# Down weights loaded four rows to a partition, and gate and up columns read four apart, in the expert stage of a two-layer backbone

## What is computed

```python
def expert_block(args):
    xblk, e = args
    hid = jax.nn.silu(xblk @ w_gate[e]) * (xblk @ w_up[e])   # [rows, 1024] @ [1024, 512], twice
    return hid @ w_down[e]                                    # [rows, 512] @ [512, 1024]
```

## Time and profile before

| What | Value |
|---|---|
| Median of 3 runs | 1149.04 us (1146.02 to 1150.01) |
| The profiled execution's own time | 1149.13 us |
| Its span, first to last instruction | 1147.1 us |
| PE busy | 1044.6 us (91%) |
| DVE busy | 621.8 us (54%) |
| ACT busy | 206.4 us (18%) |
| HBM read over the span | 314.36 MB |
| Mean granted clock of TensorE, share of full | 0.976 |

### The profile page before, as it was taken

One profiled execution on the slowest core, in us unless ns is written; L12 is line 12 of the kernel. 1 busy time (PEld: TensorE's weight loads), 2 busy tenths in 40 slices (PEclk: granted clock), 3 DMA queues, 4 the chain that ended last, 5 costly groups with the idle time before them and its releaser, 6 DMA issues.

```text
span 1147.1 us, 36219 instructions
## 1 busy us (share of the span) xinstructions
PE 1044.6 (91%) x14841; PEld 651.5 (57%) x14842; DVE 621.8 (54%) x1596; ACT 206.4 (18%) x543; POOL 140.6 (12%) x215
## 2 busy tenths in 40 slices
PE   4899989999698989999996999999988999999977
PEld 1344445554244767777773444444446777777752
DVE  1278877874358434444442886653584444444426
ACT  1212255550111000000001511021120000000010
POOL 0001100000001212122223000000012111221221
PEclk9999999999799999999997999999999999999998
DMA  8997952239534999999968994883349999999575
GB/s 319 350 345 273 340 196 74 74 147 241 179 122 169 372 421 415 421 374 418 426 266 305 336 352 159 300 310 105 118 167 382 420 414 381 376 406 424 185 298 193
DMA packets 97733, 331.91 MB, mean 289 GB/s; under 512 B 15593, under 2 KB 28305, under 8 KB 89361
## 3 DMA queue, kind: packets, MB, share of 16 engines
q1 hardware_dynamic: 66672, 289.05, 65.6%
q10 hardware_dynamic: 24672, 22.74, 6.0%
q0 software_dynamic: 6336, 19.41, 4.6%
HBM read 314.36 MB, written 25.18 MB: 296 GB/s over the span
## 4 chain that ended last, share of the span: by engine, by line
PE 70%; DMA 12%; DVE 8%; issue 3%; ACTq 2%; SPq 2%; ACT 2%; DVEq 0%; POOLq 0%
PE PS L1630 20%; PE PS L1640 12%; PE PS L1732 9%; PE PS L1425 8%; PE PS L1544 7%; DMA ring<-in_e_down_dram 5%; PE PS L1447 4%; DMA expert_rows<-RE 3%; PE PS L1473 3%; DMA RFW<-in_ln_b_dram 2%; PE PS L1459 2%; DMA ring<-in_a_wqkv_dram 2%; ACTq L601 1%; PE PS L1474 1%; PE PS L1688 1%
## 5 line engine op out<-in xcount | busy, mean ns | idle before, releaser
L1630 PE MATMUL PS<-ring,RE 128*32 128x128 f32 x6912 | 210.1, 273 | 12.3 <-issue 9.4
L1630 PEld LDWEIGHTS PS<-ring,RE 128*32 128x32 f32 x6912 | 194.6, 110 | 31.4 <-issue 22.7
L1217 DVE TENSOR_TENSOR RE<-RE,PS 128x64 f32<-128x64 f32 x160 | 35.4, 221 | 174.9 <-ACT RE L722 174.3
L1640 PE MATMUL PS<-ring,RE 128*32 128x256 f32 x1504 | 109.5, 387 | 10.2 <-DMA ring<-in_e_down_dram 4.8
L722 ACT ACTIVATE RE<-PS 128x64 f32<-128x64 f32 x160 | 35.7, 223 | 461.0 <-PE PS L1630 436.2
L1544 PE MATMUL PS<-ring,UR 128*128 128x512 f32 x256 | 115.0, 604 | 0.8 <-ACT UR L612 0.8
L1732 PE MATMUL PS<-ring,UR 128*128 128x512 f32 x256 | 111.1, 593 | 0.9 <-ACT UR L766 0.9
L1630 PE MATMUL PS<-UR,RE 128*32 128x128 f32 x3200 | 95.7, 273 | 3.5 <-issue 3.3
L1425 PE MATMUL PS<-ring,UR 128*128 128x512 f32 x224 | 98.2, 592 | 0.5 <-DMA ring<-in_a_wqkv_dram 0.5
L1630 PEld LDWEIGHTS PS<-UR,RE 128*32 128x32 f32 x3200 | 90.2, 110 | 9.9 <-issue 6.6
L531 POOL DMA_INDIRECT RE<-tokens,gcol x80 | 79.5, 993 | 60.4 <-POOL gcol L545 60.4
(11 more groups left out here) (278 smaller groups left out, 1136.0 us busy)
## 6 DMA issues: line engine op xcount, KB each, us to landing
ring<-in_w_ada_dram SPq DMA_DIRECT2D x24, 2048.0 KB
ring<-in_e_up_dram SPq DMA_DIRECT2D x22, 2048.0 KB
ring<-in_e_gate_dram SPq DMA_DIRECT2D x22, 2048.0 KB
ring<-in_e_down_dram SPq DMA_DIRECT2D x20, 2048.0 KB
RFW<-in_e_down_dram SPq DMA_DIRECT2D x12, 2048.0 KB, 19.2
UR<-in_e_up_dram SPq DMA_DIRECT2D x10, 2048.0 KB
UR<-in_e_gate_dram SPq DMA_DIRECT2D x10, 2048.0 KB
expert_rows<-RE ACTq DMA_DIRECT2D x320, 32.0 KB
```

The costliest lines, as they stand in the source:

```text
L1217: V_.tensor_tensor(hid[:, cut], gs[:, cut], PS[:, h, 64:128], ALU.mult).then_inc(loop, 1)
L1630: ins = mm(PS[BLK * q:BLK * q + BLK, h, 0:P].rearrange("p (g b i) -> p g b i", g=2, b=2), xT[:, k, :], wgu[:, :, k, 2 * h:2 * h + 2, q, :] ...
L1640: ins = mm(PS[BLK * q:BLK * q + BLK, 5, 0:256], hidT[:, BLK * k:BLK * k + BLK], wd[:, k, 256 * q:256 * q + 256], start=(k == 0), stop=(k = ...
```

## The change

Down rows are now loaded four consecutive ones to a partition: partition p holds rows 4p to 4p+3, one piece of 16 KB, as gate and up have it. For the hidden columns to come out in that order, the gate and up products take column 4(32 q + i) + b where they took column 128 b + 32 q + i. The moving operand's innermost loop i thus steps by four floats (16 bytes) where it stepped by one, and the loop b outside it by one float where it stepped by 128.

```diff
@@ load_expert
-                    src = e_down[l, e].rearrange("(k p) n -> p k n", p=P)
+                    src = e_down[l, e].rearrange("(p k) n -> p k n", k=FC)
@@ the first load of the spare slot
-                             e_down[l, src].rearrange("(k p) n -> p k n", p=P)).then_inc(w_in[b], 16)
+                             e_down[l, src].rearrange("(p k) n -> p k n", k=FC)).then_inc(w_in[b], 16)
@@ expert
-                    wgu = pair.rearrange("p g (k b q i) -> p g k b q i", k=DC, b=FC, q=CG)
+                    wgu = pair.rearrange("p g (k q i b) -> p g k b q i", k=DC, b=FC, q=CG)
```

## The result

The changed kernel takes 1395.19 us (1392.55 to 1399.57, 4 runs) against 1149.53 us of the kernel before (1146.02 to 1154.22, 4 runs): a ratio of 1.2138, 95% interval 1.2083 to 1.2193. It is slower by a fifth. The forecast was 1411.

The account below looks back on a forecast made before the run. The prediction took PE, with line 1630's column stream, to bound the kernel. To 1149.1 us it added 273 for slower reads, less 11.5 given back, loads and the rest 0: 1411 us, range 1144 to 1425.

Parts of the forecast that it names:

- What bounds: Whole kernel: PE busy 91% of the span; line 1630 is a stream at 0.86 ns a column.
- The reads: Line 1630: 16-byte steps raise a column from 0.86 to 1.70 ns, bounds 0.86 to 1.84.
- The term of 273 us: Line 1630: 2528 groups, each 0.108 us longer through the slower reads, all on the path.
- What the slowing gives back: Expert stages: late-weight waits of 4.8 and 5.4 us and a slow pass of 1.3 us go, together -11.5 us.
- The 5.4 us at line 1681: Wait for the first weights after layer 0's experts, expected to go as expert blocks grow by 3.4 us.
- The loads: Down loads in 16 KB pieces gain 2%: 0 under a slowed PE, bounds 0 to -4.3 us.
- the step is free on PE: Rival at line 1630: PE hides the fetch, leaving only the loads' gain; 1145 to 1149 us, chance 0.38.
- the cover: Down loads' 4.3 us gain lies wholly under the slowed PE, so it counts 0 in the sum.
- What was to stay as it was: Down product, SiLU and transposes keep instructions, addresses and lengths: 0.
- the factor: Rival at line 1630: strided columns cost 1.6 times plain ones, 1.38 ns; 1305 us, chance 0.08.
- one memory in turn: Rival at line 1630: four side-by-side products served in turn, 3.4 ns a column; 1970 us, chance 0.04.

Follow-up runs that it names:

- e2_reads_only: Kernel before with only the change's gate and up reads (16-byte steps), down loads as before: 1396.27 us, ratio 1.2159.
- e1_loads_only: Changed kernel with the gate and up reads of before, so only the down loads differ from the kernel before: 1194.83 us, ratio 1.0397.
- e4_pairs: Changed kernel with a read's two loops swapped, taking two neighbouring floats from each 16-byte place: 1184.01 us, ratio 1.0310.
- e9_halves: Kernel before with each gate and up load issued as two, in pieces of 8 KB instead of 16: 1149.13 us, ratio 1.0005.
- e3_two_rows: Kernel before with down rows two to a partition (8 KB pieces), gate and up read in 8-byte steps: 1153.47 us, ratio 1.0033.
- e12_pairs_halves: e4_pairs with each gate and up load issued as two, in 8 KB pieces: 1137.50 us, ratio 1.0047.

## Why the prediction was right, point by point

**What bounds.** Right: PE's stream at line 1630 was the path. What it lost was paid in full, less what the slowing gave back.

**The reads.** Right in kind, a little low in size. The step took 1.70 ns a column from DVE's rows; PE has 1.81, inside the bounds of 0.86 to 1.84. The term of 273 us is 291.9 in the page, 18.9 more. That a fetch costs a time and not a factor, the ground for choosing between 1411 and 1305, is borne out by the table above: PE's 1.81 ns is DVE's price (1.67 to 1.84) and not 1.6 times PE's own 0.86. Of the note on cachelines in the Trainium skill (SBUF — State Buffer, "Door 1"), the first half agrees with the trace: each new line pays, and two accesses to one line absorb it (0.90 ns). The second, that 4 fp32 are strided for free, does not: a step of 3 fp32 already costs 1.37 ns and one of 4 costs 1.81.

**What the slowing gives back.** Too small: -11.5 us stood there, of waits for down weights and for the first weights after layer 0. The runs have -48.5. Of these, 31.7 us are idle time before expert products, of which the page of before puts 19.0 under "issue"; the 4.8 us of waits for down weights went as said. The other 16.8 us are line 1640's, for whose length the prediction had only 1.3 us. Some of its passes were slow in the kernel before, as this one of 3.47 us, behind a stop of 2.45 us and at a granted clock of 0.53:

```profile
405.93 3.47 PE L1640 MATMUL PS<-RFW,RE 128*32 128x256 f32 x32 [2.45 <-issue]
...
405.90:409.30 3.40, 3.37 (x36) 1.89 (x40) 0.77 (x3) 0.22 (x1) 0.42 (x1) 0.53 1.06 430
```

In the changed kernel no pass takes more than 2.2 us from its first start to its last end, and the granted clock is 1.00 in both stages, where it was 0.98 and 0.99. What the stops of about 2 us named "issue" were, and why they vanish under a slower PE, no run shows.

The 5.4 us at line 1681 did not come back. The wait for weights is gone, but behind it stood one for DVE (line 1194) of 3.8 us, and the next wait, at line 1688 for the gathered outputs, grew from 3.39 to 5.10 us. Line 1688 before and after, and the wait between:

```profile
625.82 6.23 PE L1688 MATMUL PS<-UR,RFW 128*128 128x512 f32 x8 [3.39 <-DMA UR<-expert_rows,yidx]
...
PE PS L1681 <- DVE RE L1194: 3.8, 1, 3.8
...
746.34 6.14 PE L1688 MATMUL PS<-UR,RFW 128*128 128x512 f32 x8 [5.10 <-DMA UR<-expert_rows,yidx]
```

So the terms were 18.9 us too low and 37.0 too little given back. These errors of opposite sign leave 18.1, the distance from the forecast of 1410.6 to the profiled execution's 1392.55; that 1411 came so near 1395 is in part luck.

**The loads.** Right that they are worth nothing under the slowed PE (e2_reads_only against the change: 1396.3 and 1395.2 us). Wrong where it bounded them by 0 to -4.3 us and gave "the step is free on PE" a time of 1145 to 1149: with PE unslowed they cost 3 to 4% (e1_loads_only, e4_pairs). The failed sentence is "If the cover is gone (PE not slowed), it can shorten the 4.8 us of waits for down weights and no more." It looked at what the loads' own readers wait for, and not at who shares the DMA engines with them; the row of DVE's waits for stores stood in the trace of before with 23.3 us.

**What was to stay as it was.** SiLU, line 1217 and the transpose at line 1219 kept their 223, 221 and 245 ns (246 now). DVE's other transpose, line 1188, went from 649 to 682 ns, as also in e2_reads_only; it cost nothing here, and why is open.

**The rivals.** The free step, the factor and one memory in turn are each excluded by a measured duration: 7.59 us for 128 MATMULs, not 3.7, 5.7 or 14.

No version here beats the kernel before; e9_halves equals it, and e3_two_rows and e12_pairs_halves are within half a percent.

## What to carry to other kernels

Count how many new 16-byte places of SBUF a matmul's moving operand touches for each column, in its innermost loop above all: in fp32 up to one in two is nearly free (0.90 ns a column against 0.86), and one a column doubled the time. A step of two floats buys half of the layout for 0.3%. Pairs of neighbours buy all of it and cost PE as little, but with every load in 16 KB pieces the kernel lost 3.1%, and 0.5% once gate and up moved in 8 KB pieces. So when transfers are made coarser, look at the small transfers of other queues beside them: in these runs their latency grew with the length of the packets they met, and a chain that hung on them then set the pace.

## What was not expected of the hardware

With all expert loads in pieces of 16 KB the kernel was slower: 1184 us with nearly unchanged reads (e4_pairs), against 1149 with down in 4 KB pieces. The block period of 7.30 us in e1_loads_only is 12 x 0.61, the two queues pass 1530 and 1534 packets in eight such blocks, and shorter pieces of gate and up alone brought the ratio from 1.031 to 1.005. (The 1153 us of e3_two_rows, with down in 8 KB pieces, do not belong to this: DVE waits 11.6 us for stores there, less than the 23.3 of the kernel before, and line 1630 is busy for 322.6 us instead of 305.8.) That DMA engines alternate packet by packet between queues is what the Trainium skill says (DMA: Bandwidth & Descriptors, "Queues, rings and completion order"); these runs agree with it in the period, the counts and both runs with halves. The records do not say on which engine a packet ran, so the order of packets on one engine is argued from these numbers, not seen.
